# Selection of the top entries taken apart and spread over the prompt attention steps

## The reference

```python
sc = jnp.where((key_pos[None, :] <= pos[:, None])[None], sc, -jnp.inf)
_, idx = lax.top_k(sc, topk)                       # topk = 256
valid = idx <= pos[None, :, None]
return sparse_attend(qb, _gather_rows(k, idx), _gather_rows(v, idx), valid)
```

## Time and profile before

| | us |
|---|---|
| median of 3 runs | 3836.16 (3833.89 to 3838.16) |
| the profiled execution | 3854.01 |
| its span | 3852.3 |
| PE, DVE, ACT busy in the span | 3282.1, 1626.2, 1166.3 |
| selection of layer 0, from 789.07 to 822.68 | 33.6 |

### The profile page before, as it was taken

The page is one execution under the profiler, slowest core; times in us unless marked ns, Lnnn a source line. Parts: engine busy times, 40 slices in busy tenths (PEclk is TensorE's granted clock), DMA queues, the critical chain, the costliest instruction groups (busy, mean ns, idle before and its releaser), DMA issues.

```text
span 3852.3 us, 58640 instructions
## 1 busy us (share of the span) xinstructions
PE 3282.1 (85%) x20585; PEld 2751.5 (71%) x20585; DVE 1626.2 (42%) x3529; ACT 1166.3 (30%) x2049; POOL 257.5 (7%) x319
## 2 busy tenths in 40 slices
PE   3997677759889999999989867774889899999995
PEld 3994432325589999999979644231659799999995
DVE  3315556975343222222343355598534422222223
ACT  3122134845322202112231223185542321121121
POOL 1001022100200000000000100311020000000000
PEclk8997679979789999999989867997989899999997
DMA  5115014400411111111121320452042111111111
GB/s 174 39 38 200 5 57 152 153 23 21 160 41 39 44 49 44 44 48 43 41 51 39 136 80 24 121 164 77 12 138 61 33 44 45 48 44 44 49 36 53
DMA packets 275992, 261.21 MB, mean 68 GB/s; under 512 B 85512, under 2 KB 237566, under 8 KB 274512
## 3 DMA queue, kind: packets, MB, share of 16 engines
q1 hardware_dynamic: 244496, 155.76, 13.5%
q0 software_dynamic: 31312, 103.20, 8.4%
HBM read 249.33 MB, written 9.78 MB: 67 GB/s over the span
## 4 chain that ended last, share of the span: by engine, by line
PE 75%; DVE 9%; issue 7%; ACT 4%; DMA 4%; DVEq 0%; POOL 0%; ACTq 0%; SPq 0%; POOLq 0%
PE bank L701 52%; PE bank L665 5%; PE bank L736 2%; PE bank L1058 2%; PE bank L1084 2%; ACT arena L1382 2%; DMA weights<-in_w_ada 2%; DVE arena L1852 1%; DMA arena<-in_cache_kidx,page_idx 1%; PE bank L1141 1%; PE bank L983 1%; PE bank L881 1%; DMA arena<-in_x_sample 1%; PE bank L1106 1%; PE bank L947 1%
## 5 line engine op out<-in xcount | busy, mean ns | idle before, releaser
L701 PE MATMUL bank<-h_hi,w_hi 128*128 128x352 f32 x2784 | 904.6, 325 | 9.8 <-DVE w_lo L1491 9.8
L701 PE MATMUL bank<-h_lo,w_hi 128*128 128x352 f32 x2784 | 894.3, 321 | 0.0
L701 PE MATMUL bank<-h_hi,w_lo 128*128 128x352 f32 x2784 | 893.9, 321 | 0.0
L701 PEld LDWEIGHTS bank<-h_hi,w_hi 128*128 128x128 f32 x2784 | 523.8, 188 | 12.6 <-issue 7.9
L701 PEld LDWEIGHTS bank<-h_lo,w_hi 128*128 128x128 f32 x2784 | 524.8, 189 | 1.7
L701 PEld LDWEIGHTS bank<-h_hi,w_lo 128*128 128x128 f32 x2784 | 523.3, 188 | 0.0
L1491 DVE TENSOR_TENSOR w_lo<-weights,w_hi 128x1024 fp32r<-128x1024 f32 x188 | 230.2, 1225 | 626.1 <-ACT w_hi L1222 620.6
L701 PE MATMUL bank<-g_hi,w_hi 128*128 128x352 f32 x1392 | 453.5, 326 | 16.6 <-DVE arena L608 16.6
L701 PE MATMUL bank<-g_lo,w_hi 128*128 128x352 f32 x1392 | 450.0, 323 | 0.0
L701 PE MATMUL bank<-g_hi,w_lo 128*128 128x352 f32 x1392 | 449.7, 323 | 0.0
L665 PEld LDWEIGHTS bank<-arena 128*128 128x128 f32 (+4 forms) x1773 | 210.0, 152 | 269.4 <-issue 192.1
(11 more groups left out here) (322 smaller groups left out, 3820.6 us busy)
## 6 DMA issues: line engine op xcount, KB each, us to landing
weights<-in_w_ada SPq DMA_DIRECT2D x64, 512.0 KB, 6.9
weights<-in_w_gate SPq DMA_DIRECT2D x44, 512.0 KB
weights<-in_w_up SPq DMA_DIRECT2D x44, 512.0 KB, 3.8
weights<-in_w_in SPq DMA_DIRECT2D x72, 256.0 KB, 3.5
arena<-in_w_ada SPq DMA_DIRECT2D x32, 512.0 KB
weights<-in_w_down SPq DMA_DIRECT2D x32, 512.0 KB, 3.8
arena<-in_w_ada SPq DMA_DIRECT2D x8, 1024.0 KB, 18.1
weights<-in_w_down SPq DMA_DIRECT2D x16, 384.0 KB, 3.3
```

The source lines that it names most:

```text
L701: mm = pe.matmul(bank[:, 0:TC], wt[:, w], xt[:, x], start=(k + m == 0), stop=(k == n_k - 1 and m == 2))
```

## The change

Only the row set of tile 7 (j = 5), which the first four steps need, is made before the attention; also the two parts of the sample's that need no waiting, its tie count and its entries above the threshold, the latter into a tile of its own. The other row sets follow in the order j = 4, 3, 2, 1, 0, sample. Their DVE operations stand one at a time at the end of the steps (two each at steps 0 and 1), and ACT's copies at the head of the steps 2, 6, 10, 14, 18 and 22. Each has its wait: DVE's `logits` of a new tile for that tile's mask, PE's first mask of the sample for the last copy. PE no longer waits for fence 7. The scratch tiles are now R(5) to R(8), and `cum` is also the result. Since these are the buffers of the first four gathers of cached values, POOL now waits for the last copy before it issues them.

```diff
-SEL_ORDER = (6, 0, 1, 2, 3, 4, 5)
+SEL_ORDER = (5, 4, 3, 2, 1, 0, 6)
+SEL_STEP = {0: ((1, 0), (1, 1)), 1: ((1, 2), (1, 3))}
+for _m in range(2, 7):
+    for _k in range(4):
+        SEL_STEP[4 * _m - 6 + _k] = ((_m, _k),)
...
+        O_EQ, O_CUM, O_GT, O_EQS = (R(5 + n) for n in range(4))
...
                     if n < 4:
-                        pool.wait_ge(s_kv_used, l * 64 + 8 + K_TILES)
+                        pool.wait_ge(neg_ready, l * 7 + 7)
...
                 count(PASSES, "earlier_seg", M_RAW + 1)
-                ended(pe, l, 7)
...
                     if p >= MASK_AT:
+                        if p == MASK_AT:
+                            pe.wait_ge(neg_ready, l * 7 + 7)
                         mask(p - MASK_AT)
...
                 for p in range(32):
+                    if p % 4 == 2 and p < 24:
+                        negated(p // 4 + 1)
                     turned(p)
...
+                def select(m, k):
...
+                    if k == 0:
+                        if m:
+                            dve.wait_ge(sel_ready, l * 7 + m)
+                        step(dve.tensor_scalar(eq, sc, thr[:, j:j + 1], None, ALU.is_equal))
+                    elif k == 1:
+                        if m:
+                            dve.wait_ge(neg_ready, l * 7 + m)
+                        step(dve.tensor_tensor_scan(cum, eq, eq, 0.0, ALU.add, ALU.max))
+                    elif k == 2:
+                        step(dve.scalar_tensor_tensor(out=eq, in0=cum, scalar=need[:, j:j + 1], in1=eq, op0=ALU.is_le, op1=ALU.mult))
                     else:
...
+                        dve.scalar_tensor_tensor(out=cum, in0=sc, scalar=thr[:, j:j + 1], in1=eq, op0=ALU.is_gt, op1=ALU.add).then_inc(sel_ready, 1)
...
+                def select_sample(k):
...
+                    eq, cum = S(O_EQS, TOK), S(O_CUM, TOK)
+                    if k == 0:
+                        dve.wait_ge(neg_ready, l * 7 + 6)
+                        step(dve.tensor_tensor_scan(cum, eq, eq, 0.0, ALU.add, ALU.max))
+                    elif k == 1:
+                        step(dve.scalar_tensor_tensor(out=eq, in0=cum, scalar=need[:, 6:7], in1=eq, op0=ALU.is_le, op1=ALU.mult))
+                    elif k == 2:
+                        dve.tensor_tensor(cum, eq, S(O_GT, TOK), ALU.add).then_inc(sel_ready, 1)
...
+                step(dve.tensor_scalar(S(O_EQS, TOK), score(6), thr[:, 6:7], None, ALU.is_equal, ALU.add, accum_out=S(M_RAW + 1, 1)))
+                dve.sem_inc(count_raw, 1)
+                for k in range(4):
+                    select(0, k)
+                step(dve.tensor_scalar(S(O_GT, TOK), score(6), thr[:, 6:7], None, ALU.is_gt))
...
+                    if i == 0 and b > 1:
+                        dve.wait_ge(neg_ready, l * 7 + NB - b)
...
+                    for m, k in SEL_STEP.get(p, ()):
+                        if m < 6:
+                            select(m, k)
+                        else:
+                            select_sample(k)
```

More of the change, by code:

```diff
@@ L1391, in _, with negated @@
                             A.done(act.activation(S(O_KT[h % 3], 512), bank[:, :], ACT.Copy))
-                for m, j in enumerate(SEL_ORDER):
+                def negated(m):
+                    j = SEL_ORDER[m]
                     act.wait_ge(sel_ready, l * 7 + m + 1)
-                    act.activation(neg_s if j == 6 else score(j), S(R(20 + m % 2), TOK if j == 6 else P * (j + 3)), ACT.Copy, bias=-BIG, scale=BIG).then_inc(neg_ready, 1)
+                    act.activation(neg_s if j == 6 else score(j), S(O_CUM, TOK if j == 6 else P * (j + 3)), ACT.Copy, bias=-BIG, scale=BIG).then_inc(neg_ready, 1)
+                negated(0)
                 ended(act, l, 7)
@@ L1917, in _ @@
                 Dr.done(dve.tensor_scalar(S(R(24, 2048), 2 * NS), bank[:, 0:2 * NS], HD ** -0.5, None, ALU.mult))
[L1919 to L1924, removed]
-                    else:
[L1926 to L1933, removed]
-                    dve.scalar_tensor_tensor(out=sel, in0=sc, scalar=thr[:, j:j + 1], in1=eq, op0=ALU.is_gt, op1=ALU.add).then_inc(sel_ready, 1)
-                    dve.wait_ge(sel_ready, l * 7 + m + 1)
@@ new lines, in select @@
+                def select(m, k):
+                    j = SEL_ORDER[m]
+                    sc, n = score(j), P * (j + 3)
+                    eq, cum = S(O_EQ, n), S(O_CUM, n)
+                    if k == 0:
[8 more added lines that the diff above has]
+                        step(dve.scalar_tensor_tensor(out=eq, in0=cum, scalar=need[:, j:j + 1], in1=eq, op0=ALU.is_le, op1=ALU.mult))
+                    else:
+                        dve.scalar_tensor_tensor(out=cum, in0=sc, scalar=thr[:, j:j + 1], in1=eq, op0=ALU.is_gt, op1=ALU.add).then_inc(sel_ready, 1)
@@ new lines, in _ @@
+                step(dve.tensor_scalar(S(O_EQS, TOK), score(6), thr[:, 6:7], None, ALU.is_equal, ALU.add, accum_out=S(M_RAW + 1, 1)))
[3 more added lines that the diff above has]
+                step(dve.tensor_scalar(S(O_GT, TOK), score(6), thr[:, 6:7], None, ALU.is_gt))
+                dve.wait_ge(count_sum, (l + 1) * (PASSES + 1))
+                step(dve.tensor_tensor(need[:, 6:7], need[:, 6:7], XB[:, 0:1], ALU.subtract))
```

## The result

| | before | after |
|---|---|---|
| median, us | 3837.16 (3833.89 to 3840.54, 4 runs) | 3794.84 (3786.26 to 3800.07, 4 runs) |
| profiled execution, us (span) | 3854.01 (3852.3) | 3800.07 (3797.7) |

The ratio is 0.9885 [0.9869, 0.9901], 42.3 us faster (38 to 50 by the interval). The forecast was 3790.5, 45.7 us faster. A second measurement of the same two kernels gave 0.9882 [0.9863, 0.9901].

What follows compares the result with a forecast made beforehand. DVE alone was taken to bound the selection while PE waits, with DVE room in the attention. Per layer 27.14 us go and 4.30 return: 22.84, 45.7 for both, 3836.16 to 3790.5 us; forecast 3785 to 3797, 8-in-10 range 3781 to 3806.

Steps and rivals of the forecast that it cites:

- The front, 25.16 us a layer: Selection before the attention, tie count to memset behind the fence: 8.45 of 33.61 us stay, 25.16 go.
- PE's early logits, 1.98: First eviction behind the fence: DVE's wait of 1.98 us for PE's first logits goes in each layer.
- Step 0, 2.27, and step 1, 0.04: First two attention steps: moved DVE work outlasts DVE's waits by 2.27 and 0.04 us a layer.
- the clock rises a step or two later: Rival, first attention steps: a step at PE's lower clock costs 5.3 us; one a layer makes 3801; 15%.
- cost 0: PE's clock at the attention's start: the same 12 us at 1.2 GHz as before, no added cost.
- Steps 2 to 17, 0: Attention steps 2 to 17: one moved operation each, covered by DVE's wait there; cost 0.
- Step 18, 1.33: Attention step 18: the sample's scan of 2.36 us against a wait of 1.03 costs 1.33 us.
- Steps 20 and 22, 0.35 and 0.31: The sample's sum at step 20 costs 0 to 0.35 us, ACT's copy at step 22 0.31, between 0 and 0.68.
- The gathers, 0: Value gathers waiting for the last copy in step 22: four to seven at once, ahead of their use, cost 0.
- The rival that every inserted operation costs more: Rival, moved operations in the attention steps: 22 operations at 0.3 us extra, 6.6 a layer, 3804; 12%.
- Nothing is hidden: Rival, attention steps: evictions are the bound and moved work only changes place; 1.7 a layer gained, 3833; 4%.
- more is hidden: Rival, attention steps: slack in ACT and PE or an earlier clock rise hides everything; 27.14 and nothing back, 3782; 10%.

Runs made afterwards that it cites:

- its two near copies: The kernel before without PE's wait for fence 7, 3834.45 us, ratio 0.9987; and with the value gathers late, 3839.05 us, ratio 0.9998.
- the third set: Four kernels run together: the change unaltered 3792.85 us, with 896-column equality and scan inside the logits 3788.93, with gathers spaced 3796.26, with both edits 3789.59.
- the kernels with 8 columns: The change with every moved DVE operation cut to 8 columns; 3811.12 us, ratio 0.9899.
- with fillers: The change with five pairs of matmuls in step 0 whose results nobody reads, to keep PE busy; 3814.43 us, ratio 0.9903.
- the first and the third set: The first set: kernel before unaltered 0.9999, without PE's fence wait 0.9987, with late gathers 0.9998; the change with PE's fence kept 0.989.
- the second set: Four variants of the change: 8-column operations 3811.12 us, equality and scan inside the logits 3809.76, that plus sets spread by wait size 3814.15, useless matmuls 3814.43.

## Why the prediction came out right, step by step

- **The front, 25.16 us a layer.** 33.61 became 8.46: 25.15. Cover by ACT's copy held.
- **PE's early logits, 1.98.** 2.41 - 0.80 = 1.61 came in the change, 1.7 in the kernel that took away the fence alone. The eviction now waits 0.38 us for DVE's own copy of the causal mask, which the wait for PE had covered. I had asked what is late next only for PE.
- **Step 0, 2.27, and step 1, 0.04.** This is the term that was too small. Over six layers of the change (its two profiles and the one with spaced gathers: 17.50, 19.74, 19.97, 17.38, 19.50, 19.88) logits 1 to 3 take 19.0 us in the mean, over eight layers of before and its two near copies (13.45, 13.68, 14.90, 13.69, 14.83, 14.28, 13.51, 14.89) 14.2: 4.8 us a layer against 2.31. With the kernel that kept PE's fence (16.33, 19.67) the change's mean is 18.7. The scan is as costly as forecast (3.30 - 0.94 = 2.36), and with no fall of the clock that would be all, as in the layer with 16.33.

  The rest is the first rival, "the clock rises a step or two later", at about half of the price of 5.3 that it gave for one step. It had been put down as a second way for the case to go, and "cost 0" for the clock as the forecast. Both are half true: the clock rose at the same work as before, and then fell again in the wait that the change had put there. The sentence in the prediction that this idle time "falls right where the clock rose" had the mechanism and gave it no price. The rule of the Trainium skill ("TensorE: Matmul & The Clock Gate", "HAM oscillation — how this bites in real kernels"), which the prediction set aside because of the 1.00 over 837 to 870, holds here in a small form: the waits for DVE that the change left alone are 0.94 us in this stretch, the new one is 3.30. That it is the wait is shown in the third set side by side (four layers with the wait fell, four with only 0.94 did not), and by the kernels with 8 columns (wait 0.99, 13.5 us) and with fillers (no wait, clock 1.00). It does not always fall: of the eight layers with this wait it did in seven. What decides the eighth is open.
- **Steps 2 to 17, 0.** 86.74 against 86.49 us: 0.25 for 16 steps, and 0.24 with operations of 8 columns. So no operation stuck out of its wait.
- **Step 18, 1.33.** 8.48 against 7.02: 1.46.
- **Steps 20 and 22, 0.35 and 0.31.** Logits 20 to 24 took 11.33 against 11.70 us, 0.37 less. The sum of 1.21 us and ACT's copy cost nothing: the steps behind the long scan make up for a little of it.
- **The gathers, 0.** Nothing in the first and the third set: the late ones alone gave 0.9998, the spaced ones no gain. PE does wait for gathers at its value product, 6.3 us in layer 0 of the change, but before did too (5.2 in its second profile), and the sample's part is no longer for it. In the second set the stall of 5.2 to 5.7 us a layer lies exactly where they run, and it moved with them when the last copy moved. Before, only four went together ahead of fence 8 (3.09 us of POOL in the window of the selection). So the change most likely has a cost there that the forecast had not. It was not measured on the change itself, and its cause is only argued.
- **The sum.** Tie count to logits 24 became 21.4 us shorter in layer 0 and 19.4 in layer 1, 40.8 in all where 45.7 was forecast; the medians say 42.3. The 4.9 us between come from steps 0 and 1 (17.50 - 13.45 and 19.74 - 13.68, 10.1 us where 4.6 was forecast: 5.5), the first eviction (2 x 0.4) and steps 2 to 17 (0.5), less 2 x 0.9 that steps 18 to 22 cost less than forecast.
- **Some of the nearness is luck.** From the tie count to fence 8 the mean of four layers is 192.6 us before and 170.5 in the change: 22.1 a layer, close to the 22.84. But 1.1 of it comes from logits 28 to 31, which the forecast did not touch: 8.7 us when the clock stays up to their end, 10.1 to 10.8 when it falls earlier. All four layers of the change had 8.7, of the four of before only one. Whether the change does that isn't shown; the kernel with PE's fence kept had 10.09 once.
- **The rival that every inserted operation costs more** (6.6 us a layer) is refuted by the 0.25 us of steps 2 to 17. It counted 22 operations; five sets of four and three of the sample's are 23. "Nothing is hidden" is refuted by the gain itself, "more is hidden" by logits 1 to 3, and "the clock does not come back" by the windows, 0.99 and 1.00 from 819 on. DVE's idle time of "50 of 114 us" is 114 - 60.09 = 54.
- **Profile against median.** I carried the 17.85 us between the profile of before and its median over as a constant. The sample's stage shows that 11 of it lie in the longer sample's part, which the second set has too and the medians' runs, by their level, had not. To take it off came out right, though the reason was not known.

## What to carry to other kernels

Work that fits an engine's waits is free only up to the length of each wait; put the longest operation where the partner engine has work queued, and split it between evictions rather than behind the last one. When PE has just come back to the upper clock, price a new wait of some 3 us at what the next step costs at the lower clock too, not only at its own length. And judge a change in more than one place: bursts of gathers that cost nothing in two sets of runs went with a stall of some 10 us in another. Compare stages of two profiles before believing their spans: here a fifth of the difference in span (11.1 of 54.6 us) lay in a stage that the change doesn't touch.

## What the hardware showed that was not expected

- A single wait of 3.03 to 3.30 us, right behind the rise from 1.2 to 2.4 GHz, put PE back to the lower level in seven of eight layers. In two of them the next pair of logits still ran at the upper level (1.13 us) and the 16 transposes took 3.61; in the other five the pair took 2.08 and the transposes 3.67. In the eighth the clock stayed up. With a wait of 0.94 to 0.99 us at the same place it stayed up in all 18 layers traced.
- While seven gathers ran, DVE stood still for 5.4 us and ACT for 6.6 (4.95 where the gathers ran five steps earlier), "remote" in the trace, in all four kernels of one set; the same kernel in another set did not. In both, the transfer engines were nearly full from 935 to 938 us. The queues (packets, MB, share of 16 engines) from 935 to 938 us, first in the set with the stall, then in the one without:
```profile
q0 software_dynamic: 306, 1.12, 100.8%
```
```profile
q0 software_dynamic: 309, 1.14, 97.8%
q14 instruction: 1, 0.01, 0.6%
```
  With the stall the instruction queue's packet came only after 938. That instructions wait behind the gathers is a reading that fits both, not one that a run here has shown: the DVE went on at 934.22, ahead of that packet. PE's 12 stops "issue" in the sample's part of the first profile of before, at 274 GB/s (277 without the stops, in the second profile), may be the same thing: they too come only where the second set ran and in that profile.
